# Two tiles of the attention's output projection, begun among the units of the memory heads

## The reference

```python
h = rms_norm(x, pre_norm[l]); proj = h @ w_in[l]
# 6 differential heads: two score matrices each (width 32), 512 keys
p = softmax(s1) - lam * softmax(s2);  oa = rms_norm(p @ v, diff_subln[l]) * (1 - lambda_init) * silu(dgate)
# 6 GQA heads: one score matrix (width 64), 512 keys
ob = (softmax(q @ k.T * scale) @ v) * silu(ggate)
# 4 memory heads: one score matrix (width 64), 256 keys
om = (softmax(mq @ mk.T * scale) @ mv) * silu(mgate)
y = concatenate([oa, ob, om]) @ w_out[l]        # the output projection, 1024 x 1024
x = x + rms_norm(y, post_norm[l])
```

## Time and profile before

| | |
|---|---|
| time, median of 3 runs | 2844.84 us (2834.31 to 2849.65) |
| the profiled execution | 2845.66 us, span 2843.9 us |
| TensorE busy | 2727.4 us, 96% |
| VectorE busy | 1479.4 us, 52% |
| ScalarE busy | 1113.6 us, 39% |
| GpSimd busy | 590.3 us, 21% |
| mean granted TensorE clock | 0.973 |
| from a layer's first memory scores to the projection's first matmul | 41.54 us, in both layers |

### The profile page before, as it was taken

How to read it: one execution, slowest core, us unless ns; L and a number is a source line. 1 busy time by engine, 2 the same in 40 slices (tenths; PEclk the granted TensorE clock), 3 DMA queues, 4 the chain that set the end, 5 groups by cost and what they waited for, 6 DMA issues and landing times.

```text
span 2843.9 us, 35878 instructions
## 1 busy us (share of the span) xinstructions
PE 2727.4 (96%) x13734; PEld 2236.1 (79%) x13734; DVE 1479.4 (52%) x2048; ACT 1113.6 (39%) x1816; POOL 590.3 (21%) x504
## 2 busy tenths in 40 slices
PE   6999999999999999999899999999999997999998
PEld 6766688766788888888798888887888885888887
DVE  5478446576465542478364442465432774644423
ACT  3348634366543422323342222352222477422222
POOL 1030422112258900136030000156000200200000
PEclk9998989989899999999999999999999998999999
DMA  3320014210034423444323323346323441233232
GB/s 129 115 74 1 16 34 133 85 34 1 18 90 133 135 96 92 140 119 144 104 71 92 102 80 92 110 141 222 103 81 97 156 147 68 78 93 93 85 92 71
DMA packets 305580, 267.68 MB, mean 94 GB/s; under 512 B 44355, under 2 KB 296172, under 8 KB 301868
## 3 DMA queue, kind: packets, MB, share of 16 engines
q1 hardware_dynamic: 300348, 240.93, 27.4%
q0 software_dynamic: 2800, 20.25, 1.8%
q10 hardware_dynamic: 2304, 4.79, 0.6%
HBM read 238.95 MB, written 26.98 MB: 94 GB/s over the span
## 4 chain that ended last, share of the span: by engine, by line
PE 76%; DVE 10%; ACT 5%; POOL 3%; DVEq 3%; issue 2%; DMA 1%; POOLq 1%; SPq 0%; ACTq 0%
PE bank L396 21%; PE bank L398 21%; PE bank L397 21%; PE bank L1868 3%; PE bank L1856 2%; PE bank L1827 1%; DVE WL L382 1%; ACT WH L377 1%; DVE XL L456 1%; POOL MBB L757 1%; POOL MBA L757 1%; DVE X L557 1%; DVE work L553 1%; DVE stats L2188 1%; PE bank L1264 1%
## 5 line engine op out<-in xcount | busy, mean ns | idle before, releaser
L396 PE MATMUL bank<-XH,WH 128*128 128x512 f32 (+1 forms) x2400 | 900.7, 375 | 33.6 <-DVE WL L382 13.6
L397 PE MATMUL bank<-XL,WH 128*128 128x512 f32 (+1 forms) x2400 | 885.9, 369 | 0.0
L398 PE MATMUL bank<-XH,WL 128*128 128x512 f32 (+1 forms) x2400 | 885.9, 369 | 0.0
L382 DVE TENSOR_TENSOR WL<-raw,WH 128x2048 fp32r<-128x2048 f32 (+1 forms) x212 | 453.0, 2137 | 534.1 <-ACT WH L377 533.9
L377 ACT ACTIVATE WH<-raw 128x2048 fp32r<-128x2048 f32 (+1 forms) x212 | 370.1, 1746 | 476.6 <-PE bank L398 476.1
L396 PEld LDWEIGHTS bank<-XH,WH 128*128 128x128 f32 x2400 | 454.1, 189 | 127.5 <-DVE WL L382 18.9
L397 PEld LDWEIGHTS bank<-XL,WH 128*128 128x128 f32 x2400 | 455.0, 190 | 84.3 <-issue 3.3
L398 PEld LDWEIGHTS bank<-XH,WL 128*128 128x128 f32 x2400 | 453.8, 189 | 83.7
L396 PE MATMUL bank<-HH,WH 128*128 128x512 f32 (+1 forms) x792 | 294.3, 372 | 0.0
L398 PE MATMUL bank<-HH,WL 128*128 128x512 f32 (+1 forms) x792 | 292.7, 370 | 0.0
L397 PE MATMUL bank<-HL,WH 128*128 128x512 f32 (+1 forms) x792 | 292.4, 369 | 0.0
(11 more groups left out here) (402 smaller groups left out, 3655.7 us busy)
## 6 DMA issues: line engine op xcount, KB each, us to landing
raw<-in_ffn_w_dram SPq DMA_DIRECT2D x88, 1024.0 KB, 5.4
raw<-in_ffn_w_dram SPq DMA_DIRECT2D x64, 704.0 KB, 4.6
raw<-in_w_in_dram SPq DMA_DIRECT2D x24, 1024.0 KB, 5.2
MM<-mm_scr SPq DMA_DIRECT2D x12, 1152.0 KB, 7.5
raw<-in_w_out_dram SPq DMA_DIRECT2D x8, 1024.0 KB, 5.1
raw<-in_cv_w_in_dram SPq DMA_DIRECT2D x8, 1024.0 KB, 5.4
mm_scr<-MBA POOLq DMA_DIRECT2D x6, 1152.0 KB, 4.7
mm_scr<-MBB POOLq DMA_DIRECT2D x6, 1152.0 KB, 4.6
```

The costliest lines, as they stand in the source:

```text
L382: dve.tensor_tensor(WL[:, slot, 0:n * P], raw[:, slot, 0:n * P], WH[:, slot, 0:n * P].bitcast(F32), ALU.subtract).then_inc(l_done, 1)
L396: pe.matmul(out, WH[:, slot, c:c + P], h, start=start, stop=False)
L397: pe.matmul(out, WH[:, slot, c:c + P], l, start=False, stop=False)
L398: return pe.matmul(out, WL[:, slot, c:c + P], h, start=False, stop=stop)
```

## The change

In both attention layers:

- tiles 0 and 1 of the output projection no longer begin behind the last values. Their steps k = 0 to 5 are put one by one into TensorE's turns 50 to 61, after the scores: tile 0 in even turns, tile 1 in odd ones (`MIX_PART`, `mix_part`). Steps 6 and 7 of both come behind the last values (`mix_end`), then tiles 2 and 3 as before.
- the four tiles use banks 7, 2, 4 and 5. So all heads' values use bank 6, and the first half of a head waits for `outputs(h - 1)`. From unit 48 on, scores rotate over banks 3, 0 and 1 only.
- the norms are put in at unit 42, and `MIX_AT` makes operands 0 to 4 in turns 45 to 49, 5 in turn 57 and 6 in turn 65.

No instruction is added or removed.

```diff
+        def out_pe(pe, s, b, j, arrive, mh=XH, ml=XL, rows=range(KD), banks=range(4), first=None):
+            if first:
+                first()
+            else:
+                pe_block256(pe, b, 0, j, mh, ml, arrive=arrive, rows=rows)
+            pe_block256(pe, b + 1, 1, j + 2, mh, ml, rows=rows, banks=banks[2:])
...
-        NORM_U = 48
+        NORM_U = 42
+        MEM_U = 48
...
-        MIX_AT = {53: 0, 54: 1, 55: 2, 56: 3, 57: 4, 58: 5, 66: 6}
+        MIX_AT = {45: 0, 46: 1, 47: 2, 48: 3, 49: 4, 57: 5, 65: 6}
+        MIX_PART = {50 + n: (n % 2, n // 2) for n in range(12)}
+        OUT_BANKS = (7, 2, 4, 5)
...
+        def score_bank(u, i):
+
+            m = score(u, i)
+            return bank[m % 4 if u < MEM_U else (3, 0, 1)[(m - M_MEM) % 3]]
...
-                    if m >= 4:
+                    acc = score_bank(u, i)[:, 0:keys]
+                    if u >= MEM_U:
+                        pe.wait_ge(ss(s, "e"), at(s, "e", m - 2))
+                    elif m >= 4:
                         pe.wait_ge(ss(s, "e"), at(s, "e", m - 3))
...
-                if h >= 2 and half == 0:
-                    pe.wait_ge(ss(s, "o"), at(s, "o", h - 1))
+                if h >= 1 and half == 0:
+                    pe.wait_ge(ss(s, "o"), at(s, "o", h))
...
-                out = bank[6 + h % 2][:, cols]
+                out = bank[6][:, cols]
...
+            def mix_part(o, k):
+
+                if o == 0:
+                    pe.wait_ge(ss(s, "mixl"), at(s, "mixl", k + 1))
...
+                mm = mm3(pe, bank[OUT_BANKS[o]][:, :], (0, k * 256 + o * P), PRr[:, k, :], PRr[:, GATES[k], :],
+                         k == 0, k == KD - 1)
+                if k == KD - 1:
+                    mm.then_inc(mm_done, 1)
+
+            def mix_end():
+                for o in range(2):
+                    for k in range(6, KD):
+                        pe.wait_ge(ss(s, "mixl"), at(s, "mixl", k + 1))
+                        mix_part(o, k)
...
+                if u in MIX_PART:
+                    mix_part(*MIX_PART[u])
```

More of the change, by code:

```diff
@@ L398, in mm3, with pe_block256 @@
             return pe.matmul(out, WL[:, slot, c:c + P], h, start=False, stop=stop)
-        def pe_block256(pe, b, slot, j, mh, ml, n=T, arrive=None, rows=range(KD), middle=None):
+        def pe_block256(pe, b, slot, j, mh, ml, n=T, arrive=None, rows=range(KD), middle=None, banks=None):
             pe.wait_ge(l_done, b + 1)
@@ L405, in pe_block256 @@
                     middle()
-                acc = bank[2 * slot + o][:, 0:n]
+                acc = bank[banks[o] if banks else 2 * slot + o][:, 0:n]
                 if not isinstance(j, int) or j + o >= 4:
@@ L1087, in out_sp @@
                 load_block(sp, b + i, i % 2, raw3(i % 2, KD), w3[:, :, i * 256:(i + 1) * 256])
-        def out_pe(pe, s, b, j, arrive, mh=XH, ml=XL, rows=range(KD)):
-            for i in range(2):
-                pe_block256(pe, b + i, i, j + 2 * i, mh, ml, arrive=arrive if i == 0 else None, rows=rows)
+        def out_pe(pe, s, b, j, arrive, mh=XH, ml=XL, rows=range(KD), banks=range(4), first=None):
[4 more added lines that the diff above has]
+            pe_block256(pe, b + 1, 1, j + 2, mh, ml, rows=rows, banks=banks[2:])
             for h in range(2):
@@ L1151, in out_act, with out_dve @@
             turn_act(act, s, sqr, evict, b + 4, step + 8, 6, middle)
-        def out_dve(dve, s, b, j, step, Y, gain, bias=None):
+        def out_dve(dve, s, b, j, step, Y, gain, bias=None, banks=range(4)):
             for i in range(2):
@@ L1156, in out_dve @@
                     dve.wait_ge(mm_done, step + o + 1)
-                    acc = bank[2 * i + o % 2]
+                    acc = bank[banks[o]]
                     if bias is None:
@@ L1561, in score @@
             return SCORE0[u] + i + (3 if u >= NORM_U else 0)
+        M_MEM = score(MEM_U, 0)
+        def score_bank(u, i):
+            m = score(u, i)
+            return bank[m % 4 if u < MEM_U else (3, 0, 1)[(m - M_MEM) % 3]]
         def by_dve(u):
@@ L1821, in scores @@
                                           for name, c, w in ((q, t * P, P), (k, k0, keys))]
-                    acc = bank[m % 4][:, 0:keys]
-                    if m >= 4:
+                    acc = score_bank(u, i)[:, 0:keys]
+                    if u >= MEM_U:
+                        pe.wait_ge(ss(s, "e"), at(s, "e", m - 2))
+                    elif m >= 4:
                         pe.wait_ge(ss(s, "e"), at(s, "e", m - 3))
@@ L1869, in values @@
                 mm.then_inc(ss(s, "pv"), 1)
+            def mix_part(o, k):
+                if o == 0:
+                    pe.wait_ge(ss(s, "mixl"), at(s, "mixl", k + 1))
+                if k == 0:
+                    if o == 0:
+                        pe.wait_ge(l_done, b0 + 14 + 1)
+                        pe.wait_ge(acc_read, j0 + 28)
+                    else:
+                        pe.wait_ge(ss(s, "e"), at(s, "e", M_MEM))
+                mm = mm3(pe, bank[OUT_BANKS[o]][:, :], (0, k * 256 + o * P), PRr[:, k, :], PRr[:, GATES[k], :],
[7 more added lines that the diff above has]
+                        mix_part(o, k)
             for u in range(len(UNITS) + LAG_V):
@@ L1879, in attn_pe @@
                     transposes(u - LAG_T)
-            out_pe(pe, s, b0 + 14, j0 + 28, (s, "mixl"), PRr, PRr, GATES)
+            out_pe(pe, s, b0 + 14, j0 + 28, None, PRr, PRr, GATES, OUT_BANKS, mix_end)
         def attn_act(act, s):
@@ L2019, in exps @@
                     m = SCORE0[u] + i
-                    act.activation(E[:, m % SLOTS, 0:nk * P], bank[score(u, i) % 4][:, 0:nk * P], ACT.Exp,
+                    act.activation(E[:, m % SLOTS, 0:nk * P], score_bank(u, i)[:, 0:nk * P], ACT.Exp,
                                    bias=stats[:, 1, m % 8:m % 8 + 1],
@@ L2187, in maxima @@
                     dve.wait_ge(ss(s, "s"), at(s, "s", score(u, i) + 1))
-                    ins = dve.tensor_reduce(stats[:, 1, c:c + 1], bank[score(u, i) % 4][:, 0:nk * P], AX, ALU.max,
+                    ins = dve.tensor_reduce(stats[:, 1, c:c + 1], score_bank(u, i)[:, 0:nk * P], AX, ALU.max,
                                             negate=True)
@@ L2220, in outputs @@
                 dve.wait_ge(ss(s, "pv"), at(s, "pv", 2 * h + 2))
-                acc = bank[6 + h % 2][row:row + 64, :]
+                acc = bank[6][row:row + 64, :]
                 if h == 6:
@@ L2260, in attn_dve @@
             mix_low(KD - 1)
-            out_dve(dve, s, b0 + 14, j0 + 28, s0 + 28, YA, post)
+            out_dve(dve, s, b0 + 14, j0 + 28, s0 + 28, YA, post, banks=OUT_BANKS)
         c_rows = [G1[:, i].rearrange("p g s h -> p g (s h)") for i in range(2)]
```

## The result

The changed kernel takes **2846.54 us** (median of 20 runs, 2844.42 to 2854.61), the kernel before 2844.54 us beside it (20 runs, 2826.62 to 2849.65). The ratio is 1.0022, 95% interval 1.0012 to 1.0033: slower by 0.2%, a little, but clear of no change. The forecast was 2836.2 us, faster by 0.3%, in a range of 2823 to 2852. The time lies within the range, but the sign is wrong, and behind the near zero stand three large terms that cancel.

What follows compares the result with a forecast made beforehand. TensorE ends the chain for 76% of the span, slow at low clock in the memory heads. Per layer -1.5 - 6.5 + 2.7 + 0.35 + 0.2 = -4.75, two layers -9.5 us from 2845.66: 2836.2 us, range 2823 to 2852.

Steps and rivals of the forecast that it cites:

- C: One bank for the values: start waits for the previous head's copy; +2.7 us a layer in differential heads, 0.35 in GQA.
- rival 2: More clock falls, in differential heads and at the memory stretch's end: +4 to +12, 2840 to 2848 us; chance 0.19.
- rival 3: Differential heads stay at half clock, TensorE sets the pace; two in each layer, +26 gives 2862 us; chance 0.08.
- A: Memory stretch: projection pieces keep the clock up and fill gaps; 40.0 us instead of 41.54, 1.5 shorter a layer.
- rival 4: Pieces don't lift the clock in the memory stretch, which stays low; +14 a layer, 2874 us; chance 0.06.
- B: End of the attention: third tile begins 4.7 us after the last values instead of 11.2, -6.5 us a layer.
- D: Three banks for the scores, which wait for exponentials of three units earlier, not four: put at nothing.
- E: Norms six units earlier: TensorE's gap shrinks to 0.1 or 0.2 among GQA units; counted as +0.2 us a layer.

## Why the prediction was wrong

**C failed by its size, and that turned the sign.** The step that failed is the price of TensorE's wait: the forecast's sum counted it as VectorE's stall alone, 2.7 us a layer, and put the clock's answer at nothing, left to rivals 2 and 3. The differential heads became 10.9 and 7.4 us longer. The wait was found (1.7 forecast, 2.04, 1.72, 1.69 and 1.83 measured in the first layer), its four heads too, and the stall alone has its price (0.7 for the reduce against 0.65, 2.7 a layer against 2.7 at full clock). What it missed is the step from a wait to a clock, 9.2 and 5.2 us.

Rival 2 priced a single fall at 1.6 us at most, from the one fall in the earlier trace rows. That was near: the kernel before's falls cost 1.3 and 0.95 us, and the three of the changed kernel's second layer 5.2 us together. What was off in the forecast is how often they come and how long they last: six of the eight waits are followed by a fall, and in the first layer one lasts 10.2 us and one 6.8. The second layer is rival 2's mechanism. The two long falls of the first layer are rival 3's mechanism, TensorE at half clock sets the pace. In all the clock took 14.4 us in the two layers, about half of the 26 us that rival 3 gave. Rival 2's times (2840 to 2848) are where the kernel landed. The Trainium skill ("TensorE: Matmul & The Clock Gate", "A second HAM failure mode: psum-queue depth-cycling") describes a clock that goes up and down because TensorE idles briefly between groups of matmuls as it cycles through PSUM banks; the first layer of the changed kernel agrees with it (0.50, 1.00, 0.50, 1.00, 0.50 above), and I had weighed it too lightly because the trace of before did not yet show it.

Part of the closeness in time is luck: A, below, came out 2.1 us a layer better than forecast, 4.2 us in all, and hid as much of C's error.

**A was near in its size and wrong in its reason.** 37.95 us for 40.0, a saving of 3.6 us for 1.5, the clock at 1.00, a piece 0.80 us for 0.85, a pair of units 4.17 us for 4.5. But the clock does not stay up because of the pieces. It never falls once the norms are gone from the stretch: 28.93 us without a piece, and 28.93 + 12 x 0.80 = 38.5 is already near the stretch with them. The estimate of 29.6 us for a stretch without gaps and at full clock stood in the working; the question whether the gaps might be the cause did not, beyond "the gaps are small". Nor did the projection's stream behind the stretch raise the clock of before, as A and the argument against rival 4 took it: it was up 2.0 us ahead of the projection's first matmul (378.61), among the last transposes and values:

```profile
376.60:378.61 2.01, 1.84 (x10) 1.34 (x9) 0.89 (x2) 1.12 (x3) 0.00 (x0) 1.00 0.00 0
```

The sentence on the Trainium skill (Part 4 of the same page, transposes do not count as busy in the way matmuls do) was of no use to tell: the same transposes run at 1.00 in one kernel and at 0.50 in another.

**B was right.** -6.4 us for -6.5, and the wait for VectorE's low part 1.57 us for 1.8:

```profile
387.83 0.58 PE L396 MATMUL bank<-PRr,WH 128*128 128x512 f32 x1
...
390.45 0.47 PE L396 MATMUL bank<-PRr,WH 128*128 128x512 f32 x1 [1.57 <-DVE PRr L2279]
...
392.62 0.40 PE L396 MATMUL bank<-PRr,WH 128*128 128x512 f32 x1
```

But A and B together are no gain of the pieces. They take twelve times three matmuls out of a stream that does three in 0.70 us, 8.4 us, and put them into a stretch that grows by 38.06 - 28.93 = 9.1 us for them; the end gets shorter by 6.4 us and not by 8.4, since the 1.57 us are uncovered. That is 0.7 + 2.0 = 2.7 us a layer lost, 5.5 of the 6.9 us between the two medians.

**D held:** behind the pieces' start no wait of the scores is to be seen; the waits of 0.49 and 0.43 us ahead of the last values are for copies, the second for the one bank of the values (0.2 forecast).

**E was booked on the wrong side.** It stood as a cost of 0.2 us. It is the source of the whole gain, 22.8 and 21.6 us in the two runs that move the norms, because that takes the two gaps out of the memory units. One wait of the bank was missed there, at turn 47:

```profile
347.55 1.97 PE L1883 MATMUL bank<-PT,Vg 128*128 128x256 f32 x8 [1.01 <-DVE PR L2266]
```

So the change is, by the separate runs: norms early -22.8 us (2843.59 to 2820.78), pieces with three score banks +6.9, one value bank +18.9, together +3.0, where +2.0 was measured. The steps follow each other from the kernel before to the changed one, so their sum is no test of them; the 1.0 us between 3.0 and 2.0 is that between two medians of the kernel before.

## What to carry to other kernels

Price a new wait of TensorE twice, once as a stall and once as a fall of the clock, and look at who sets the pace at half clock; here the second price was 9.2 and 5.2 us in the two layers, for a stall of 2.7. Give the clock a term of its own in the sum when a wait is new, not only a rival. When a stretch is slow and fully busy, look at the gaps just ahead of it before adding work to it, and move whatever makes them. When a buffer is given away, the reader's place in its own engine's turn decides whether anyone waits: putting the copy first was worth as much as the second bank.

## What the runs showed of the hardware

The memory units can run at either level of the clock with TensorE busy all the time. The same instructions of TensorE take 28.93 us at 1.00 from end to end, and 41.54 to 44.56 us with 20 to 24 us of them at 0.50. One gap of 1.99 us brought the clock down for 3.4 us in one layer and 6.8 in the other; a second, of 1.45 us and 8.9 us after the first had ended, brought it down for 24 us, until 1.7 us ahead of the projection, and for 20 in the other layer. Gaps of 0.3 to 0.4 us did nothing there. A wait of 1.01 us in the GQA heads was followed by a fall in one of four layers (those of the changed kernel and of the run with filled waits), and waits of 1.69 to 2.04 us in the differential heads of the changed kernel in six cases of eight. So one execution, or one layer, does not tell what a gap costs.

What brings a fallen clock back early or late stays open. The two layers of the run with one value bank alone have the same instructions and the same gaps where the clock falls, and were back after 24 and 10 us, without pieces. With pieces among the units both layers were back after 10 us.
